# The gather of the first expert's rows: token rows as TensorE's weights, the one-hot matrix moving

## The reference, cut to what matters

```python
def moe_swiglu(x, w_router, w_gate, w_up, w_down):
    logits = (x @ w_router).astype(jnp.float32)
    top_val, top_idx = lax.top_k(logits, TOP_K_EXPERTS)
    gate = jax.nn.softmax(top_val, axis=-1)
    combine = jnp.einsum('btk,btke->bte', gate, jax.nn.one_hot(top_idx, N_EXPERTS, dtype=jnp.float32)).astype(x.dtype)
    out = jnp.zeros_like(x)
    for e in range(N_EXPERTS):
        out = out + combine[..., e:e + 1] * swiglu(x, w_gate[e], w_up[e], w_down[e])
    return out
```

## Time and profile before

| | |
|---|---|
| median of 3 runs | 1494.31 us (1493.27 to 1495.09) |
| profiled execution, its own time | 1490.39 us |
| its span, first to last instruction | 1488.5 us |
| mean granted TensorE clock | 0.975 |
| PE busy | 1413.7 us (95%) |
| DVE busy | 488.2 us (33%) |
| HBM traffic | 260 GB/s over the span |

### The profile page before, as it was taken

One profiled execution on the slowest core, in us unless ns is written; L12 is line 12 of the kernel. 1 busy time (PEld: TensorE's weight loads), 2 busy tenths in 40 slices (PEclk: granted clock), 3 DMA queues, 4 the chain that ended last, 5 costly groups with the idle time before them and its releaser, 6 DMA issues.

```text
span 1488.5 us, 38226 instructions
## 1 busy us (share of the span) xinstructions
PE 1413.7 (95%) x17306; PEld 963.0 (65%) x17306; DVE 488.2 (33%) x1048; ACT 216.5 (15%) x481; POOL 188.6 (13%) x227
## 2 busy tenths in 40 slices
PE   7999989999999999987989999999999999999994
PEld 5767877777777777777644656656565665646442
DVE  2399331111023756674451213013121202212232
ACT  3044120000002512232220000000000000000001
POOL 4137200000000325124221000000000000000100
PEclk9999999999999999998989999999999999999997
DMA  9434024334433320103759999999999999999998
GB/s 372 148 135 159 15 115 154 129 127 156 156 104 122 128 100 3 60 3 136 298 234 381 390 414 413 404 414 403 414 403 413 413 403 413 381 415 407 407 397 318
DMA packets 90459, 389.12 MB, mean 261 GB/s; under 512 B 12544, under 2 KB 15328, under 8 KB 90043
## 3 DMA queue, kind: packets, MB, share of 16 engines
q1 hardware_dynamic: 82048, 365.84, 62.8%
q0 software_dynamic: 4832, 17.17, 3.2%
q10 hardware_dynamic: 3418, 3.68, 0.7%
HBM read 378.74 MB, written 7.91 MB: 260 GB/s over the span
## 4 chain that ended last, share of the span: by engine, by line
PE 86%; DVE 8%; DMA 2%; issue 1%; ACT 1%; SPq 0%; DVEq 0%
PE bk L1627 29%; PE bk L1644 15%; PE bk L1110 12%; PE bk L795 9%; PE bk L1123 6%; PE bk L1542 2%; PE bk L1025 2%; PE bk L1217 1%; DMA part<-in_moe_down 1%; DVE left L2196 1%; DVE tops L2194 1%; PE bk L1138 1%; DMA ring<-in_weights 1%; PE bk L1159 1%; DVE sc_p L2181 1%
## 5 line engine op out<-in xcount | busy, mean ns | idle before, releaser
L1627 PE MATMUL bk<-part,xe 128*32 128x352 f32 x6144 | 458.9, 459 | 2.4 <-DVE xe L2664 2.4
L1627 PEld LDWEIGHTS bk<-part,xe 128*32 128x32 f32 x6144 | 244.1, 110 | 212.3 <-issue 169.1
L1644 PE MATMUL bk<-part,hidT 128*32 128x256 f32 x4224 | 232.4, 379 | 0.7 <-DMA part<-in_moe_down 0.6
L1644 PEld LDWEIGHTS bk<-part,hidT 128*32 128x32 f32 x4224 | 153.5, 110 | 77.4 <-issue 2.1
L1110 PE MATMUL bk<-xn,ring 128*128 128x288 f32 x704 | 174.0, 411 | 2.8 <-DVE xn L2272 2.8
L1110 PEld LDWEIGHTS bk<-xn,ring 128*128 128x128 f32 x704 | 135.5, 193 | 40.9 <-issue 3.0
L2732 DVE TENSOR_TENSOR hp<-sg,bk 128x352 f32<-128x352 f32 x48 | 37.1, 773 | 354.1 <-PE bk L1627 354.1
L795 PE MATMUL bk<-mx,ring 128*128 128x288 f32 x384 | 98.4, 415 | 0.0
L795 PE MATMUL bk<-xg,ring 128*128 128x288 f32 x336 | 88.8, 424 | 3.1 <-DMA ring<-in_weights 3.0
L795 PEld LDWEIGHTS bk<-mx,ring 128*128 128x128 f32 x384 | 73.4, 194 | 21.2 <-issue 0.8
L1123 PE MATMUL bk<-hid,ring 128*128 128x288 f32 x352 | 85.5, 406 | 0.0
(11 more groups left out here) (547 smaller groups left out, 1274.8 us busy)
## 6 DMA issues: line engine op xcount, KB each, us to landing
part<-in_moe_gate SPq DMA_DIRECT2D x136, 704.0 KB, 19.1
part<-in_moe_up SPq DMA_DIRECT2D x136, 704.0 KB, 17.9
part<-in_moe_down SPq DMA_DIRECT2D x128, 704.0 KB, 15.3
ring<-in_weights SPq DMA_DIRECT2D x121, 512.0 KB, 4.3
ro<-in_weights SPq DMA_DIRECT2D x8, 512.0 KB, 5.9
expert_rows<-ye ACTq DMA_DIRECT2D x7, 384.0 KB, 7.1
Ss<-in_states SPq DMA_DIRECT2D x1, 2048.0 KB, 8.6
out_wkv_sample<-Ss SPq DMA_DIRECT2D x8, 256.0 KB, 2.4
```

The source lines that it names most:

```text
L1627: last = mm(banks[g][32 * c:32 * c + 32, 0:FQ], xe[:, k, 32 * g:32 * g + 32], parts[PART_OF[ph]][:, FH * k + FQ * c:FH * k + FQ * c + FQ], ...
L1644: last = mm(down_bk[g // 2][32 * q:32 * q + 32, 256 * (g % 2):256 * (g % 2) + 256], hidT[:, half, g, 32 * m:32 * m + 32], parts[PART_OF[ph ...
```

## The change

The gather swaps its operands. PE's weights become the token rows themselves, 128 tokens by 128 features of xr (of the third tile its 32 real rows), and pick moves, all 96 slots at a time. The output then has features on partitions and slots along the columns, as xe wants it, so DVE's transposes go, and the multiply with the gain reads PSUM and writes xe directly. It is done in two halves of four feature chunks: PE increments xe_mm after each half, and DVE multiplies the first half while PE works on the second. POOL now waits for xe_mm 2.

```diff
         def gather():
 
-            for i in range(3):
-                in_parts = xr[:, i].rearrange("p (k q d) -> p q k d", k=KC, q=4)
-                for g in range(3):
-                    for q in range(4):
-                        last = mm(gate_bk[g // 2][32 * q:32 * q + 32, 256 * (g % 2):256 * (g % 2) + 256],
-                                  pick[:, i, 32 * g:32 * g + 32], in_parts[:, q],
-                                  start=i == 0 and g != 1, stop=i == 2, skip_group_check=True)
-            last.then_inc(xe_mm, 1)
+            for k in range(KC):
+                for i, (t0, tn) in enumerate(TILES):
+                    last = mm(gate_bk[k // 4][:, CAP * (k % 4):CAP * (k % 4) + CAP], xr[0:tn, i, P * k:P * k + P], pick[0:tn, i],
+                              start=i == 0, stop=i == 2)
+                if k % 4 == 3:
+                    last.then_inc(xe_mm, 1)
...
         def columns_in():
-            dve.wait_ge(xe_mm, 1)
-            for g in range(3):
-                last = V.transpose(xe[:, :, 32 * g:32 * g + 32],
-                                   bk[g // 2][:, 256 * (g % 2):256 * (g % 2) + 256].rearrange("p (k s) -> p k s", k=KC))
-            last.then_inc(xe_ok, 1)
-            dve.wait_ge(xe_ok, 1)
-            V.tensor_tensor(xe[:], xe[:], row_gain.unsqueeze(2).broadcast_to([P, KC, CAP]), ALU.mult).then_inc(xe_ok, 1)
+            for half in range(2):
+                ks = slice(4 * half, 4 * half + 4)
+                dve.wait_ge(xe_mm, half + 1)
+                V.tensor_tensor(xe[:, ks], bk[half][:, 0:4 * CAP].rearrange("p (k s) -> p k s", k=4),
+                                row_gain[:, ks].unsqueeze(2).broadcast_to([P, 4, CAP]), ALU.mult).then_inc(xe_ok, 1)
...
-        pool.wait_ge(xe_mm, 1)
+        pool.wait_ge(xe_mm, 2)
```

## The result

Over 16 runs of each kernel the median went from 1493.18 to 1500.44 us. The ratio of after to before is 1.0048, with a 95% interval of 1.0034 to 1.0063: 7.2 us slower (5.1 to 9.4). The forecast was slower by 5.05 us, at 1499.3 us in a range of 1494.5 to 1502.0. The forecast of the time (1.1 us off) looks better than that of the difference (2.2 us off): it started from a median before of 1494.31 us, and over the 16 runs that median is 1493.18.

What follows compares the result with a forecast made beforehand. PE paces the kernel, with a serial stretch from gather to expert 0. That stretch 3.45 us longer plus 1.6 us behind it made 5.05 us slower, a median of about 1499.3 us, range 1494.5 to 1502.0.

Steps and rivals of the forecast that it cites:

- The stretch: Gather's start to expert 0, a strict series of PE and DVE: 12.4 us against 8.95, 3.45 us longer.
- Streaming is equal: In the gather, moving columns take 2304 columns' worth of time both before and after the change.
- wide loads set the pace: In the gather, a 128-column load outlasts 96 moving columns: 0.213 us an instruction at half clock, about 0.112 at full.
- The price of a chunk: In the gather, six matmuls with two row-count changes: about 1.45 us at half clock, 0.88 at full.
- The clock stays at 0.50 for the whole gather: PE's granted clock does not return until the experts run, so the gather takes 11.6 us.
- rival (a): The clock comes back within the gather: +0.8 us (1495.1) or +2.2 us (1496.5); chance 0.20.
- the stretch of wide loads from 36.12: Evidence for half clock: PE loaded 128-column weights back to back to 39.70, and right after the clock was 0.50.
- DVE's part: Behind the gather, transposes go and one half-multiply is hidden; 384 columns from PSUM remain, about 0.55 us.
- Behind it: Start of expert 0 at half clock loses 2.2 us; PE's wait for the last expert's matrices shrinks 0.6: 1.6 us.
- POOL is covered: POOL's scaling, stores and gathers start some 5 us later, hidden by its 23.93 us wait for DVE's row numbers.
- Rival (b): In the gather, loads hide and row-count changes are free; DVE's 1.5 us saving remains: 1492.8; chance 0.06.
- Rival (c): In the gather, loads never overlap: 0.37 us an instruction, gather 17.9 us, kernel 1505.6; chance 0.03.

Runs made afterwards that it cites:

- full_rows: Kernel after, but the third token tile takes all 128 rows, so the row count never changes; ratio to the kernel before 1.0006.
- strips_32: Features-on-partitions gather with 32-column loads in four strips, third tile at 32 rows; one execution, no ratio; gather 10.26 us.
- full_rows_busy_early: Kernel after with full-row third tile, eight unread matmuls ahead of the gather, and columns_in right behind pick; ratio to the kernel before 0.9976.
- after: The kernel with the change (operands swapped, third tile at 32 rows), against the kernel before: 1500.44 us, ratio 1.0048.
- after_again: The kernel after, unchanged, a second execution under the profiler; gather repeats to 0.01 us, clock back 4.59 us into expert 0.
- after_busy: Kernel after plus eight matmuls nobody reads, placed where PE idles ahead of the gather; ratio to the kernel before 1.0045.
- strips: Kernel after, but weights of 128 tokens by 32 features, four matmuls side by side, third tile with 128 rows; ratio to the kernel before 0.9991.
- tiles_outer: Kernel after with loops swapped, token tile outside, so the row count changes once; ratio to the kernel before 1.0008.
- before_busy: Kernel before plus eight matmuls nobody reads, placed where PE idles ahead of the gather; ratio to the kernel before 0.9997.
- before_busy_early: Kernel before plus eight unread matmuls ahead of the gather, and columns_in right behind pick; ratio to the kernel before 0.9988.

## Why the prediction was right, and where a size was off

- **The stretch is serial and paces the kernel**: right. 6.05 + 1.9 us found by place, 7.2 us in the medians.
- **Streaming is equal, wide loads set the pace at 0.213 and 0.112 us**: right; full_rows shows both numbers (5.31 / 25 = 0.212, 2.78 / 25 = 0.111).
- **The price of a chunk, 1.45 us at half clock**: this term was mis-sized. It is 1.77, and eight times 0.32 is 2.6 us, all of the gather's excess over the forecast 11.6. I built it from transposes that change row count (line 811) plus three instructions. The loads' starts say where the two differ. The change to 32 rows was right: 0.50 us (at line 811 0.555, less the 0.05 that I took off). The change back to 128 rows also takes 0.50, and at line 811 it takes 0.24 (loads at 6.85 and 7.09 us of the kernel before): that is 0.26 of the 0.32. The transpose of 32 rows moves 32 columns, the new matmul 96; I took 0.05 off for 96 columns instead of 128 and added nothing for 96 instead of 32. Its loads are shorter too (0.18 to 0.22 us, here 0.28 to 0.34). Which of the two makes the change back cheap there no run separates. strips_32 fits a price that grows with the width of the load. At full clock a chunk is 1.0 us, not 0.88.
- **The clock stays at 0.50 for the whole gather**: right, in both executions, against rival (a). The ground that I gave was only the nearest rows, and one of the two misled: the stretch of wide loads from 36.12 made wide loads a suspect, and they do not hold the clock down (full_rows, full_rows_busy_early). What does is the third tile's 32 rows with their changes (after, after_again, after_busy, strips_32), which is the other row, line 811. So the choice was right partly by luck: for the same loads without the changes the first row would have forecast the wrong clock.
- **DVE's part, 0.55 us left**: right, 0.57.
- **Behind it, 2.2 us at half clock less 0.6 of the wait for the down matrices**: 1.9 to 2.3 us (half of 3.83 and of 4.59), right; but the wait shrank by 0.2 only, and 0.6 was taken off.
- **POOL is covered**: right, by a wait of 25 us.
- **Rival (b)**, loads that hide, is out for this kernel: the gather took 14.2 us. strips is the kernel in which they do hide, by being narrow; (b)'s gain was 1.5 us, and strips' ratio of 0.9991 is 1.3 us.
- **Rival (c)**, loads that never overlap: 14.2 us is below its 15, and the instructions within a set of one shape follow at 0.213 us, so loads and matmuls do overlap there. But across a change of row count they don't, fully. The rule of the Trainium skill ("TensorE: Matmul & The Clock Gate", "Part 3: Packing small matmuls — row/col tiling"), that loads overlap with matmuls only where row groups differ, does not hold here: matmuls that use the same rows overlap with the next load, and it is at a change of rows that overlap is lost. (The change from 128 to 32 rows is no clean test of the rule's other half, as both use rows 0 to 31.)

Left open: what in the mixed chunks holds the clock down. The gaps between shapes and the 32-row matmuls themselves come together in every run whose clock stayed down through the gather. tiles_outer has 32-row matmuls with one change, and its clock fell right behind them; that would speak for the matmuls, but the clock also fell at the start of expert 0 in before_busy and before_busy_early, which have none.

## What to carry to other kernels

A small remainder tile inside the inner loop can cost more than padding it to full rows: keep the shape of consecutive matmuls the same, or put the odd tile in a pass of its own. Swapping which operand is the weight left the moving columns equal here (2304) and changed the width of the loads; where few columns move, narrow strips side by side gave the same output at close to the price of the moving columns (in strips 5.50 us for 140 instructions, four at a time, is 0.157 us a set, and 96 columns are 0.160). And before an engine on the path is made faster, look at how long its consumer is still busy with other work: here there was 0.7 us of slack (774.4 to 775.13), and the rest of the gain had to wait until DVE's order was changed.

## What was not expected

- Work without idle time in PE's row doesn't guarantee the 2.4 GHz level: PE was busy for 14.18 us at 0.50 (after), and lost 1.00 after 5.16 us of its own busy gather (after_busy). The weight loads' row did have a gap at each change of shape: loads were under way for 11.37 of the 14.18 us, where in full_rows (771.50 to 776.80) they never paused.
- Multiplying 96 rows of zeros more made the gather 6.1 us shorter (14.2 to 8.1).
- Eight useless matmuls keep the clock up through the router and shorten the slot counts (line 1569 before) from 1.94 to 1.18 us.
